# Scan mixer: lag tables assembled in four parts during the first FFN, two chunk tables loaded behind the first eviction, log/exp table loaded ahead of the norm

## The reference

```python
x = x + mix(rms_norm(x, g))          # mix: fourier, scan, attention, fourier
x = x + swiglu(rms_norm(x, g), w_gate_up, w_down)
# scan mixer: 64 groups of 16 channels, 64 complex states each, forward and backward
dt = exp(log_dt); lam_bar = exp(lam * dt); b_bar = (lam_bar - 1) / lam * B
h[t] = lam_bar * h[t-1] + b_bar @ u[t]      # and the same from the end backwards
y = Re(C_fwd @ h_fwd) + Re(C_bwd @ h_bwd) + d * u
out = val * sigmoid(gate),  val, gate = split(gelu(y) @ w_glu)
```

## Time and profile before

| | us |
|---|---|
| median of three runs | 3273.17 (3272.41 to 3273.86) |
| the profiled execution | 3274.13 |
| its span, first to last instruction | 3272.1 |
| PE busy | 2963.7 (91%), mean granted clock 0.935 |
| DVE, ACT, POOL busy | 1560.0, 1078.6, 247.6 |

### The profile page before, as it was taken

The page is one execution under the profiler, slowest core; times in us unless marked ns, Lnnn a source line. Parts: engine busy times, 40 slices in busy tenths (PEclk is TensorE's granted clock), DMA queues, the critical chain, the costliest instruction groups (busy, mean ns, idle before and its releaser), DMA issues.

```text
span 3272.1 us, 39214 instructions
## 1 busy us (share of the span) xinstructions
PE 2963.7 (91%) x15982; PEld 2392.9 (73%) x15982; DVE 1560.0 (48%) x2411; ACT 1078.6 (33%) x1651; POOL 247.6 (8%) x228
## 2 busy tenths in 40 slices
PE   6999994579999989989999799999899998898977
PEld 5787883567888878778787478887788886665745
DVE  5775662844434433443434654343543444534444
ACT  4332331253222224434535332122432223522233
POOL 2332220110000000000000200000200000100000
PEclk9999997789999989989999899999999999987868
DMA  3244437443543222112122322222122222111000
GB/s 110 87 146 141 137 132 226 150 129 100 129 125 115 98 77 69 65 68 78 61 100 81 119 90 91 103 90 90 52 93 100 97 97 86 52 40 39 14 26 26
DMA packets 109572, 305.30 MB, mean 93 GB/s; under 512 B 27232, under 2 KB 67488, under 8 KB 80080
## 3 DMA queue, kind: packets, MB, share of 16 engines
q1 hardware_dynamic: 106512, 281.83, 26.0%
q10 hardware_dynamic: 2880, 20.97, 1.8%
HBM read 265.11 MB, written 41.85 MB: 94 GB/s over the span
## 4 chain that ended last, share of the span: by engine, by line
PE 79%; DVE 8%; ACT 3%; issue 2%; POOL 1%; SPq 1%; DMA 1%; DVEq 0%; ACTq 0%; POOLq 0%
PE ps L94 78%; DVE s_ L117 2%; PE ps L99 1%; SPq L154 1%; DVE H_ L117 1%; DVE htf_ L131 1%; ACT htf_ L113 0%; ACT wh_ L113 0%; ACT hh_ L113 0%; DVE ol_ L117 0%; DVE Pm_ L117 0%; DVE nmx_ L139 0%; ACT PT_ L113 0%; ACT rs_ L113 0%; POOL oml_ L117 0%
## 5 line engine op out<-in xcount | busy, mean ns | idle before, releaser
L94 PE MATMUL ps<-hh_,wh_ 128*128 128x512 f32 x2184 | 871.4, 399 | 21.0 <-DVE hl_ L117 9.9
L94 PE MATMUL ps<-hl_,wh_ 128*128 128x512 f32 x2184 | 856.8, 392 | 0.0
L94 PE MATMUL ps<-hh_,wl_ 128*128 128x512 f32 x2184 | 856.4, 392 | 0.0
L117 DVE TENSOR_TENSOR wl_<-raw_,wh_ 128x2048 fp32r<-128x2048 f32 x209 | 480.3, 2298 | 554.3 <-ACT wh_ L113 554.3
L113 ACT ACTIVATE wh_<-raw_ 128x2048 fp32r<-128x2048 f32 x209 | 399.0, 1909 | 374.2 <-PE ps L94 361.3
L94 PEld LDWEIGHTS ps<-hh_,wh_ 128*128 128x128 f32 x2184 | 414.2, 190 | 121.5 <-issue 14.7
L94 PEld LDWEIGHTS ps<-hh_,wl_ 128*128 128x128 f32 x2184 | 414.1, 190 | 87.9
L94 PEld LDWEIGHTS ps<-hl_,wh_ 128*128 128x128 f32 x2184 | 414.5, 190 | 87.3 <-issue 3.7
L94 PE MATMUL ps<-ah_,wl_ 128*128 128x512 f32 x704 | 279.5, 397 | 0.0
L94 PE MATMUL ps<-ah_,wh_ 128*128 128x512 f32 x704 | 278.3, 395 | 0.0
L94 PE MATMUL ps<-al_,wh_ 128*128 128x512 f32 x704 | 277.7, 395 | 0.0
(11 more groups left out here) (317 smaller groups left out, 3730.3 us busy)
## 6 DMA issues: line engine op xcount, KB each, us to landing
raw_<-in_w SPq DMA_DIRECT2D x209, 1024.0 KB, 4.9
sO<-s5ce_ SPq DMA_DIRECT2D x32, 256.0 KB, 2.8
sW<-s5wt_ SPq DMA_DIRECT2D x16, 512.0 KB, 3.0
sA<-os_ SPq DMA_DIRECT2D x24, 256.0 KB, 2.2
ol_<-sA SPq DMA_DIRECT2D x24, 256.0 KB, 3.8
sT<-sK SPq DMA_DIRECT2D x8, 512.0 KB, 7.3
sB<-mk_ SPq DMA_DIRECT2D x8, 510.0 KB, 7.7
wh_<-sW ACTq DMA_DIRECT2D x3, 1024.0 KB, 5.2
```

What stands on the lines that cost most here:

```text
L94: return self.e.matmul(out, lhsT, rhs, start=start, stop=stop, skip_group_check=True)
L117: return Nothing() if self.e is None else self.e.tensor_tensor(out, a, b, op)
```

## The change

Five edits. `explogs` loads the log/exp table by itself, and each FFN calls it in its second half, between the gate/up pairs and the down projections. `same_sync` takes a part number and is called by `prep_sync` behind piece 4, 8, 12 and 16, each part on 16 groups, with a completion event for each; `sT` is laid out in four blocks. `table_load` waits for its own part. Tables 6 and 7 are loaded behind the eviction of chunks 0. `PREP_FIRST` is 23, and the `yield` in `prep_vector` moves, so that the steps of PE, ACT and SP come one call later than those of DVE and POOL that feed them.

```diff
+    def explogs(self):
+        if not self.explog and self.e is not None:
+            self.e.preload_act_table_set("natural_log_exp_and_others")
+        self.explog = True
...
         if f in (ACT.Exp, ACT.Ln):
-            if not self.explog and self.e is not None:
-                self.e.preload_act_table_set("natural_log_exp_and_others")
-            self.explog = True
+            self.explogs()
...
@@ ffn_scalar
+        if half:
+            ac.explogs()
         for m in range(8):
...
-PREP_FIRST = 22
+PREP_FIRST = 23
...
@@ prep_sync
                    P.wt[:, :, :, :].rearrange("p g r x -> p (g r x)")).then_inc(*K.lane("s5sW").up("p.sW", pc - 1))
+            if pc % 4 == 0:
+                same_sync(K, sp, pc // 4 - 1)
...
-def same_sync(K, sp):
+def same_sync(K, sp, un):
-    src = d["sK"].rearrange("q (g x) -> q g x", g=64)
-    sp.wait_ge(*K.at("p.sK", 15))
+    src = d["sK"][:, 3840 * un:3840 * un + 3840].rearrange("q (g x) -> q g x", g=16)
+    sp.wait_ge(*K.at("p.sK", 4 * un + 3))
     for t in range(8):
-        sp.dma(d["sT"][16 * t:16 * t + 16, :].rearrange("q (g x) -> q g x", g=64),
-               src[:, :, (7 - t) * 16:(7 - t) * 16 + 128]).then_inc(*K.lane("s5sT").up(*(("p.sT",) if t == 7 else ())))
+        sp.dma(d["sT"][un, 16 * t:16 * t + 16, :].rearrange("q (g x) -> q g x", g=16),
+               src[:, :, (7 - t) * 16:(7 - t) * 16 + 128]).then_inc(*K.lane(f"s5sT{un}").up(*(("p.sT", un) if t == 7 else ())))
...
@@ prep_vector
         yield
         yield
+        yield
         vb = K.mb["p.b", pc][:, 0:128].rearrange("p (s x) -> p s x", s=8)
...
-        yield
         yield
...
@@ table_load
     if name == "sT":
-        ac.wait_ge(*K.at("p.sT"))
-        src = K.d["sT"][:, 2048 * n:2048 * n + 2048]
-    else:
-        src = K.d[name][n]
+        ac.wait_ge(*K.at("p.sT", n))
...
@@ s5_scalar
     rstd_scalar(K, ac, 2)
-    for i in (6, 7):
-        table_load(K, ac, i, "used", K.first_glu - 1)
     for un in range(8):
...
+        for i in (6, 7) if un == 0 else ():
+            table_load(K, ac, i, "used", K.first_glu - 1)
         table_load(K, ac, 8 + un)
...
@@ s5_sync
     spread(len(RUNS) - 1)
-    same_sync(K, sp)
     bias_sync_in(K, sp)
```

More of the change, by code:

```diff
@@ L1092, in table_load @@
     if name == "sT":
-        ac.wait_ge(*K.at("p.sT"))
-        src = K.d["sT"][:, 2048 * n:2048 * n + 2048]
-    else:
-        src = K.d[name][n]
+        ac.wait_ge(*K.at("p.sT", n))
     if name == "sW":
         ac.wait_ge(*K.at("p.sW", 2 * n + 1))
-    ac.dma(table(K, i), src).then_inc(*K.lane(f"table{i % 8}").up("s.raw", i))
+    ac.dma(table(K, i), K.d[name][n]).then_inc(*K.lane(f"table{i % 8}").up("s.raw", i))
 def tables_early(K, ac, m):
@@ L3517, in two_model_stack @@
 def two_model_stack(nc, d):
-    for nm, shape in (("sW", [8, 128, 2048]), ("sT", [128, 4 * 2048]), ("sO", [8, 128, 2048]), ("sK", [16, 64 * 240]),
+    for nm, shape in (("sW", [8, 128, 2048]), ("sT", [4, 128, 2048]), ("sO", [8, 128, 2048]), ("sK", [16, 64 * 240]),
                       ("hx", [8, 128, 512]), ("yx", [8, 128, 512]), ("sB", [16, 128 * BN]), ("sA", [24, 128, 512])):
```

## The result

The changed kernel takes 3254.6 us (median of four runs, 3251.0 to 3259.5) against 3273.3: ratio 0.9944, interval 0.9927 to 0.9961. It is 18.7 us faster where 38.5 were forecast. The profiled execution took 3254.25 with a span of 3252.4.

The account below looks back on a forecast made before the run. Waits between the first FFN's last matmul and the scan start were taken as the bound, then DVE's scan steps. Scan start 29.4, first FFN 5.3 and later norms 3.8 summed to 38.5 us: 3234.7 us, range 3230 to 3246.

Parts of the forecast that it names:

- the landing of run 2: Before the scan: the small spread DMAs PE's chunks 2 needs land 2.3 us after issue, plus 1 us for three table loads.
- Two of the signs: Signs of a wrong prediction: spreads landing over 5 us after issue, PE's clock falling between chunks 1 and 4, DVE awaiting chunks 7.
- Rival 1: Before the scan: table loads collide with the small spread DMAs; scan starts by 560.7, gain 29.7, 3243.5 us; chance 0.18.
- The later norms: Three later norms: table load between the rstd's matmul and the Ln goes, 1.28 us each, 3.8 us in all.
- PREP_FIRST: First FFN, fourth pair: PE's stall falls from 5.26 to 2.5 us (2.8 gained), clock stays high (2.5 more); 5.3 us.
- The first table load: End of the first FFN: load moves ahead to idle ACT time, so rstd, norm and first store come 1.28 us sooner.
- rival 6: At four norms: the table switch costs more than its load, giving 3.6 us more, 3231 us; chance 0.02.
- Part 3: Last lag-table part, end of first FFN: SP's eight copies take 0.46 us each to issue, over by 517, before the store.
- rival 3: Last lag-table part holds SP at 1.50 us an issue, so the first store lands 2.6 to 7.6 later; 3237 to 3242; chance 0.06.
- rivals 2 and 5: 2: first FFN gives nothing, 3240 us, chance 0.09. 5: ACT still waits for `sT`, 3263 us, chance 0.02.
- The store: First input tile's store before the scan: issued at 520.72, landing at 525.0 instead of 529.6; bounds 523.3 and 528.3.
- Rival 4: Slower: SP's queue backs up behind the tables, 24 spread issues at 2.5 us each; 3283 us; chance 0.03.

## Why the prediction was wrong

**The step that failed** is "the three loads are issued at the same moment, and I add 1 us" for the landing of run 2. Counted as there, from the end of the last issue to chunks 2, it took 14.4 us (534.0 to 548.37) where I had 2.3 + 1. PE's chunks 2 were to stand 27.4 us behind the FFN's last matmul (542.1 - 514.65) and stood 40.1 behind it (548.37 - 508.24). Of these 12.7 us the landing is 11.1 and the store's later landing 1.2; the low clock during chunks 2 added 1.8 (5.53 - 3.76). Together that is the shortfall of 14.5: 14.9 us measured of the scan start's 29.4. Two of the signs that I had named occurred: spreads landed more than 5 us after issue, and the clock fell between chunks 1 and 4. The runs with 0, 1 and 4 MB of table loads at that moment (3.3, 7.05, 14.91 us) show the cause. I had issued exactly these loads in my own walk, and had the row of a store that took 7.61 behind two tables; I let being issued first count as a protection, and took 7.6 as the worst case although four tables, not two, would be there. Scaled with the bytes, that bound would have been 2 x 7.6 = 15.2.

**Rival 1** was the right mechanism with the wrong size. It put chunks 3's eviction at 560.7 in old times, 46 us behind the FFN; it was 51.8. With its own later-norm term intact it gave 3243.5.

**The later norms** (3.8 us) failed as a sum: in the changed kernel 3 x 1.28 came at the Ln of each, and then 1.2 us were lost in attention, 2.0 in Fourier 3. The sentence at fault is "Everything behind hangs on the rstd". What hangs on it is PE's restart, not the speed at which PE then runs. (In attention the low time of the changed kernel, 82.0 us, is not above the old 85.5, so there the 1.2 us are not explained by its sum.) With the table alone the loss took the whole gain. The 2.4 us in the mixers are not shown to belong to it: the four parts alone, without this edit, had 513.44 there, and the five other kernels with it lie between 507.5 and 510.7.

**PREP_FIRST** was right in both halves: 5.3 predicted, 5.0 measured alone, 2.4 us of stall left, and the clock stayed at the high level (low 6.9 to 0 or 1.0 us). The row that I read for the clock behind 2.3 us of idle time, 514.60:516.90, is that idle time itself; from 516.9 to 518.1 the granted clock was 1.00 too, so the reading holds. In the changed kernel it does not: behind the same 2.26 us ahead of the rstd the granted clock was 0.71 from 510.5 to 512.0, and the two matmuls took 1.44 us instead of 1.11. **The first table load** gave its 1.28 less these 0.33. From the FFN's last matmul to the Ln it took 4.7 us before and 3.5 with the table alone: one load and no more, so rival 6 did not occur. **Part 3** took 0.64 us an issue, not 0.46, and was over before the store; rival 3 did not occur, nor did rivals 2 and 5. **The store** landed in 5.53, 1.2 later than I had, of which the tables 4 and 5 are the cause: moved away, it took 2.10. **Rival 4**'s backing up of SP's queue is in the trace (16 issues in 17.96 us, 1.12 each), but off the path, as chunks 6 came later than the spreads. **Parts 0 to 2** cost PE nothing: in the first FFN it waited for nothing but that one operand. DVE had no gap at the joint steps, as predicted. The 1.3 us of Fourier 0 can't be put down to the change: in the seven kernels with `PREP_FIRST` 23, whose code is the same up to there, it lay between 105.9 and 108.2.

**Left open:** why PE's clock returns later behind a shorter idle time, what makes the mixers vary by 6 us between kernels, and why the stretch from the GLU's products to the norm is 2 to 3 us longer in four of them.

## What to carry to other kernels

When a wait is removed, list every transfer that its engine will now issue early, add up the megabytes, and add that time to each small transfer on the path that is in flight then, even one issued first. Large loads belong behind the last small transfer of a dependent chain, or well ahead of its first one; here that was worth as much as the change itself. And a shortened wait of TensorE is not gained until the granted clock behind it has been read.

## What the hardware showed

A 64 KB DMA on one queue, issued 0.6 to 1.5 us after three 1 MB loads on another, and 2.1 us before a fourth, landed with the last of them: 14.9 us after its issue, against 2.5 to 3.4 for the spreads of the same run with no load queued. The Trainium skill, DMA: Bandwidth & Descriptors, "Issuing engines are not separate DMA queues" says that such DMAs interleave on the same engines. These runs agree, and show that the small one can pay for nearly all of the large ones' bytes.

After 6.3 us of idle time TensorE ran at the 1.2 GHz level for longer than after 7.6: in Fourier 3, 17.1 to 26.5 us in all instead of 13.5, in each of the six kernels with the shorter wait, and 13.5 to 13.7 in each of the five with the longer one. Why is not shown.
